# Two halves of a sequence solved together, and output work dealt over the merge, in a two-block network on one core

## The chip, the core and the metric

One core of a Trainium2 chip runs the whole program in one launch. The time is device microseconds of that core. The kernel before was timed in three runs. A profile was taken in one more execution; rows and busy times come from that one.

## The reference, cut to what matters

One sequence of 256 positions, width 1024, goes through two layers of a first kind and two of a second kind. The change touches the first kind only. Its layer, cut:

```python
u = rms_norm(h, norm_mix_g[layer])
p_a, p_b, p_c, p_gate = split(u @ w_in[layer])
y_a = rwkv7_branch(p_a, ...)     # per head: state = state*w + (state@a) b^T + v k^T ; y = state@r ; group norm
y_b = hgrn2_branch(p_b, ...)     # gated linear attention: scores with exp of cumulative gates; rms norm
y_c = dsa_branch(p_c, cos, sin)  # index scores, top 64 keys per query, softmax attention over them
branch = einsum('bsnc,ncd->bsnd', stack([y_a, y_b, y_c]), w_branch[layer])
merged = sum(sigmoid(p_gate) * branch, axis=2)
h = h + merged @ w_o[layer]
h = h + conv_glu(rms_norm(h, norm_ffn_g[layer]), ...)
```

The recurrence of the first branch is computed by halves c of 128 positions. For each head and half, a matrix I - N (N strictly lower triangular, from the keys and decays) has to be inverted, and the right sides of half 1 need the state that half 0 leaves.

## The kernel before, in words

Every engine has one queue in program order; semaphores join them. Weights stream in pieces of four blocks through a ring (SyncE's DMAs). ScalarE writes the high part of each piece into a ring of four (`hi.upto`, `hi.more`; L1325 is the line of all its activations), POOL subtracts to get the low part (L1291), and TensorE does three matmuls per block (`mm`, L650; transposes L759). A high part can be made only when the piece four before it is used, so ScalarE stands in `hi.upto` while TensorE is in a projection. PSUM banks are taken in the order of the list of `groups1`; each name waits for the one eight places before it.

One layer of the first kind, from the end of its first projections:

1. `scores(c)`: matrices N and T of half c. VectorE (from L2049) masks them into `nn`, `xd` and `zd`.
2. Levels k = 1 to 6 (`LEVELS` is 7), which double the inverted diagonal blocks: `level_first` (16 small matmuls per level), a copy by ScalarE (`level`, into `o1`), `level_second` (X and Z), a masked merge by VectorE (`level`, L2088 and L2091; L2083 in the last). `head_scores` with `take_scores` (L2068) make the scores of two heads beside levels 1 to 4.
3. `solve(c)`: right sides R, solutions SA, outputs Y, each with a copy by ScalarE between; for half 0 also the state ST, which VectorE scales in `state` (L2100, L2102) and on which R1 and Y1 rest.

Half 0 goes first. Beside its levels TensorE has the projections Bi, Cqi, Cki, Cv, Bg0, Bg1 and the rotations, and VectorE the rotary steps, the gate's logarithms and sums (L2183 to L2227) and the index scores. Then VectorE takes the top 64 keys (`take_best`, L2143 and L2144, eight rounds per block of queries; `best_mask`), and half 1 starts with `scores(1)`. Beside half 1's levels lie the attention (`logits`, `masked_logits` L2160 and L2162, `softmax`, `probabilities` L2168 and L2170, `turn_probs`, `values`), one unit of six per level, and the pair levels of the second branch: POOL's differences and products (`level_operands`, L1304, L1305, L1309, L1310), an exponential by ScalarE (`pair_decays`), `hgrn_pairs` on TensorE (banks H0 to H7) and `take_pairs` on VectorE (L2111 to L2116). POOL begins them after the low parts of Bg1. HO is that branch's output.

After that come the group means GM and the merge: for i = 0 to 11, over branches C, B, A with four column groups each, a gate projection and an output projection on TensorE, a sigmoid by ScalarE, a product and a sum by VectorE (L2286, L2289). The outputs of branch B (`yb`) and A (`ya`) get their norms and gains from VectorE (L1847 to L2277) before merge 0's product; their high and low halves must be there at merges 4 and 8.

## Time and profile before

| | us |
|---|---|
| median of three runs | 2082.19 |
| lowest and highest | 2081.07, 2087.68 |
| profiled execution | 2088.02 |
| its span | 2086.0 |
| TensorE busy | 1904.5 (91% of the span) |
| VectorE, ScalarE, POOL busy | 1288.3, 1145.3, 1032.5 |
| mean granted clock of TensorE | 0.953 of full speed |

The profile shows each instruction with its engine, line, start and duration in one execution. Idle time of an engine stands in brackets, with what ended it. A granted clock of 1.0 is 2.4 GHz and 0.5 is 1.2 GHz. In counts of instructions a small matmul of the program stands twice.

### The profile page before, as it was taken

What the parts mean: (1) busy time and instruction counts of PE and PEld (TensorE: products, weight loads), DVE (VectorE), ACT (ScalarE), POOL (GpSimd) and SP (SyncE); (2) the same over time, 40 slices, a digit from 0 to 9 for tenths busy, and PEclk for the clock granted to TensorE, in tenths of its full rate; (3) what the DMA queues carried; (4) which work ended last, traced back from release to release, by engine and by line L of the source; (5) the groups of instructions that cost most, each with busy time, mean ns of one, the idle gap of its engine ahead of it and who ended that gap; (6) DMA issues with size and microseconds to landing.
All of it is one profiled execution on the core that took longest, in us unless ns stands there. A gap on an engine that the chain in (4) does not pass through costs nothing.

```text
span 2086.0 us, 44562 instructions
## 1 busy us (share of the span) xinstructions
PE 1904.5 (91%) x16390; PEld 1795.9 (86%) x16390; DVE 1288.3 (62%) x1943; ACT 1145.3 (55%) x1928; POOL 1032.5 (49%) x742
## 2 busy tenths in 40 slices
PE   9897888999999898788999999988899998879999
PEld 8787777999999787677999989866799997659999
DVE  4567736369933367746268973476776536777754
ACT  5645255557755644355457655665655457465543
POOL 5662258929997572257938986751200045411000
PEclk9998799999999999799999999997999999879999
DMA  6332004656665442004656654530366653205665
GB/s 213 118 116 66 2 22 127 187 152 178 187 193 167 128 130 70 6 2 117 183 153 178 187 179 136 152 97 25 102 183 200 187 162 117 71 19 151 187 187 166
DMA packets 146923, 271.20 MB, mean 130 GB/s; under 512 B 16434, under 2 KB 16947, under 8 KB 146739
## 3 DMA queue, kind: packets, MB, share of 16 engines
q1 hardware_dynamic: 145296, 264.97, 43.5%
q10 hardware_dynamic: 1442, 3.66, 0.5%
q8 instruction: 130, 2.13, 0.4%
q14 instruction: 55, 0.44, 0.1%
HBM read 267.52 MB, written 1.05 MB: 129 GB/s over the span
## 4 chain that ended last, share of the span: by engine, by line
PE 68%; DVE 13%; ACT 10%; POOL 6%; issue 2%; ACTq 0%; DMA 0%; DVEq 0%; POOLq 0%
PE bank L650 67%; ACT arena L1325 7%; POOL ring_split L1291 5%; ACT hi_ring L1325 1%; DVE arena L1848 1%; PE bank L759 1%; DVE arena L1847 1%; DVE u L1918 1%; DVE arena L2144 1%; DVE small L2143 1%; ACT L1325 1%; DVE arena L2274 0%; DVE arena L2381 0%; DVE arena L2268 0%; DVE u_split L1923 0%
## 5 line engine op out<-in xcount | busy, mean ns | idle before, releaser
L1291 POOL TENSOR_TENSOR ring_split<-ring,hi_ring 128x512 fp32r<-128x512 f32 x682 | 961.9, 1435 | 742.1 <-ACT hi_ring L1325 731.9
L1325 ACT ACTIVATE hi_ring<-ring 128x512 fp32r<-128x512 f32 x1002 | 618.2, 630 | 520.9 <-PE bank L650 498.2
L650 PE MATMUL bank<-u_hi,hi_ring 128*128 128x256 f32 (+1 forms) x2480 | 678.6, 286 | 57.2 <-POOL ring_split L1291 44.7
L650 PE MATMUL bank<-u_split,hi_ring 128*128 128x256 f32 (+1 forms) x2480 | 667.0, 282 | 1.6 <-DVE u_split L1923 1.4
L650 PE MATMUL bank<-u_hi,ring_split 128*128 128x256 f32 (+1 forms) x2480 | 666.7, 281 | 0.0
L650 PEld LDWEIGHTS bank<-u_hi,hi_ring 128*128 128x128 f32 (+1 forms) x2480 | 454.5, 189 | 72.0 <-POOL ring_split L1291 50.8
L650 PEld LDWEIGHTS bank<-u_split,hi_ring 128*128 128x128 f32 (+1 forms) x2480 | 454.0, 189 | 4.1 <-DVE u_split L1923 2.4
L650 PEld LDWEIGHTS bank<-u_hi,ring_split 128*128 128x128 f32 (+1 forms) x2480 | 455.1, 189 | 1.0
L650 PE MATMUL bank<-arena 64*64 64x64 f32 (+6 forms) x3680 | 257.9, 266 | 51.3 <-ACT arena L1325 19.5
L650 PEld LDWEIGHTS bank<-arena 64*64 64x64 f32 (+3 forms) x3680 | 223.8, 163 | 91.3 <-issue 47.0
L1956 DVE TENSOR_TENSOR ring_split<-ring,hi_ring 128x512 fp32r<-128x512 f32 x320 | 217.6, 700 | 120.0 <-ACT hi_ring L1325 116.4
L650 PE MATMUL bank<-hidden_hi,hi_ring 128*128 128x256 f32 x864 | 242.9, 281 | 9.9 <-POOL ring_split L1291 9.9
L1325 ACT ACTIVATE arena<-bank 128x512 f32<-128x512 f32 (+5 forms) x262 | 131.6, 502 | 213.3 <-PE bank L650 171.9
L650 PE MATMUL bank<-hidden_hi,ring_split 128*128 128x256 f32 x864 | 242.1, 280 | 0.0
L650 PE MATMUL bank<-hidden_lo,hi_ring 128*128 128x256 f32 x864 | 242.1, 280 | 0.0
L1325 ACT ACTIVATE arena<-arena 128x1024 f32<-128x1024 f32 (+8 forms) x205 | 156.3, 763 | 44.5 <-DVE arena L2426 16.4
L650 PEld LDWEIGHTS bank<-hidden_hi,hi_ring 128*128 128x128 f32 x864 | 162.9, 189 | 11.6 <-issue 6.4
L650 PEld LDWEIGHTS bank<-hidden_hi,ring_split 128*128 128x128 f32 x864 | 165.3, 191 | 0.0
L650 PEld LDWEIGHTS bank<-hidden_lo,hi_ring 128*128 128x128 f32 x864 | 162.9, 189 | 0.0
L650 PE MATMUL bank<-arena,cst 128*128 128x256 f32 (+2 forms) x378 | 101.5, 412 | 13.6 <-ACT arena L1325 12.9
L1847 DVE SCALAR_TENSOR_TENSOR arena<-arena 128x1024 f32<-128x1024 f32 (+3 forms) x27 | 28.6, 1061 | 118.9 <-ACT arena L1325 118.6
L1325 ACT ACTIVATE arena<-bank,par 128x256 f32<-128x256 f32 x140 | 75.2, 537 | 43.7 <-PE bank L650 40.6
(247 smaller groups left out, 2445.3 us busy)
## 6 DMA issues: line engine op xcount, KB each, us to landing
ring<-in_stream SPq DMA_DIRECT2D x1002, 256.0 KB, 2.7
par<-in_params ACTq DMA_DIRECT2D x3, 637.0 KB, 4.3
h<-in_x SPq DMA_DIRECT2D x4, 256.0 KB, 4.1
cst<-in_cst SPq DMA_DIRECT2D x1, 993.0 KB
out<-h ACTq DMA_DIRECT2D x3, 256.0 KB, 2.8
par<-in_params ACTq DMA_DIRECT2D x1, 633.0 KB, 9.0
out<-h ACTq DMA_DIRECT2D x2, 128.0 KB, 2.3
msk<-in_masks SPq DMA_DIRECT2D x1, 104.0 KB
```

The source lines that it names most:

```text
L650: ins = nc.tensor.matmul(o, l, r, start=start, stop=stop)
L759: ins = nc.tensor.transpose(bank[:, i * P:(i + 1) * P], a, ident)
L1291: G.tensor_tensor(ring_lo[:, c, :], ring[:, c, :], hi_ring[:, q % HI_RING, :].bitcast(F32), ALU.subtract).then_inc(lo_by_pool, 1)
L1325: return nc.scalar.activation(o, i, f, **kw)
L1847: C.link(V.scalar_tensor_tensor(sq, sq, -0.5, y, ALU.mult, ALU.mult))
L1848: C.link(V.scalar_tensor_tensor(buf, sq, 1.5, buf, ALU.add, ALU.mult))
L1918: ins = V.scalar_tensor_tensor(u[:, k, :], h[:, k, :], gain[:, k:k + 1], buf, ALU.mult, ALU.mult)
L1956: V.tensor_tensor(ring_lo[:, c, :], ring[:, c, :], hi_ring[:, q % HI_RING, :].bitcast(F32), ALU.subtract).then_inc(lo_by_vector, 1)
L2143: C.link(V.max(m8, work[tt][:, 0:w]))
L2144: C.link(V.match_replace(work[tt][:, 0:w], m8, work[tt][:, 0:w], TAKEN))
```

## The change

Banks, instructions and results stay the same but for their order, with these differences. `nn`, `xd`, `zd`, `o1` and `x11` get a second buffer, in room that is free at the time, so both halves can be in levels at once. TensorE goes `scores(0)`, `scores(1)`, Bi, then per level both halves' `level_first`, the scores of two heads of half 0, both `level_second`, and the work beside. Index scores move from levels 4 and 5 to level 3, the gate's logarithms to before the levels (their activations before Bi on ScalarE), its sums to level 1, top-k of block 0 to level 4, pair group 7 and HT to level 5, HS and pair group 0 to level 6. After the levels come R0, SA0, Y0, ST, half 1's head scores, R1, SA1 and Y1, spread among attention units and pair levels, in an order written out by hand on each engine. The softmax maxima and sums get two sets of four columns. In the merge, the norm and gain work on `yb` follows merges 0 to 2 and that on `ya` merges 3 to 6, instead of all going before merge 0.

The core of the diff:

```diff
@@ groups1
+    beside = {1: ["Cqi", "Rq0", "Cki"], 2: ["Rq1", "Rk", "Cv", "Rqi", "Rki"], 3: [n for n, _, _ in INDEX] + ["Bg0"], 4: ["Bg1"], 5: ["HT", "H7"], 6: ["HS", "H0"]}
@@ build
+        nn = [nn0, v3(ya, 8)]
+        xd, x11 = ([v3(a[:, o:o + 512], 8) for o in (0, 512)] for a in (flat(xx), yb))
@@ tensor
                 scores(0)
+                scores(1)
                 project_rows(["Bi0", "Bi1"], u_parts, 4)
                 for k in range(1, LEVELS):
                     level_first(0, k)
+                    level_first(1, k)
+                    head_scores(0, pair_of(k))
                     level_second(0, k)
+                    level_second(1, k)
...
+                right_sides(0)
+                logits(0)
+                solutions(0)
+                logits(1)
+                hgrn_pairs(1)
+                outputs(0)
+                state()
+                turn_probs(0)
+                head_scores(1, (0, 1))
+                values(0)
+                hgrn_pairs(2)
+                turn_probs(1)
+                head_scores(1, (2, 3))
+                logits(2)
+                values(1)
+                head_scores(1, (4, 5))
+                logits(3)
+                head_scores(1, (6, 7))
+                hgrn_pairs(3)
+                turn_probs(2)
+                right_sides(1)
+                values(2)
+                logits(4)
+                turn_probs(3)
+                hgrn_pairs(4)
+                solutions(1)
+                values(3)
+                logits(5)
+                turn_probs(4)
+                hgrn_pairs(5)
+                outputs(1)
+                values(4)
+                turn_probs(5)
+                hgrn_pairs(6)
+                values(5)
@@ scalar
+                act.wait_ge(S["hcol_in"], past["hcol_in"] + 1)
+                C.link(A(lbc, lbc, ACT.Exp), S["hcol_out"])
+                act.wait_ge(S["ls_in"], past["ls_in"] + 1)
+                C.link(A(hE, bf, ACT.Abs))
+                C.link(A(hE, hE, ACT.Exp, scale=-1.0))
+                hi.more()
+                act.wait_ge(S["hcol_in"], past["hcol_in"] + 2)
+                nc.scalar.preload_act_table_set(LN)
+                C.link(A(lnA, lnA, ACT.Ln))
+                C.link(A(ln1m, ln1m, ACT.Ln), S["hcol_out"])
+                C.link(A(hE, hE, ACT.Ln, bias=1.0), S["ls_out"])
                 for t in range(NT):
                     hi.upto("Bi0")
...
+                take_sides(0)
+                softmax(0)
+                take_solutions(0)
+                softmax(1)
+                take_outputs(0)
+                pair_decays(2)
+                take_turned(0)
+                take_values(0)
+                pair_decays(3)
+                take_turned(1)
+                take_values(1)
+                softmax(2)
+                softmax(3)
+                pair_decays(4)
...
@@ vector
+                C.link(V.tensor_tensor(lbc, p("lb0"), p("lb1"), ALU.subtract), S["hcol_in"])
+                C.link(V.tensor_scalar(hls, bf, 0.0, None, ALU.min), S["ls_in"])
                 C.link(V.memset(st, 0.0))
                 C.link(V.memset(hsc, 0.0))
                 scores(0)
+                lower_bounds()
+                scores(1)
+                gate_logs()
                 for k in range(1, LEVELS):
+                    take_scores(0, pair_of(k))
+                    for c in range(2):
+                        level(c, k, 0)
+                        level(c, k, 1)
...
+                masked_logits(0)
+                take_best(1, half_rounds // 2)
+                masked_logits(1)
+                take_best(1, half_rounds // 2)
+                probabilities(0)
+                take_pairs(1)
                 state()
+                take_scores(1, (0, 1))
+                probabilities(1)
+                take_pairs(2)
+                take_scores(1, (2, 3))
+                take_best(1, half_rounds // 2)
+                best_mask(1)
+                masked_logits(2)
...
@@ the merge on vector, after the product and sum of merge i
+                    if i == 0:
+                        refine(C, "hgrn", 2)
+                    elif i == 1:
+                        C.link(V.tensor_tensor(yb, yb, hE, ALU.mult))
+                        dve.wait_ge(S["bsg_ready"], past["bsg_ready"] + 1)
+                        gated(C, (0, 1))
+                    elif i == 2:
+                        gated(C, (2, 3))
+                        split(C, yb, yb_hi, yb_lo, S["yb_ready"])
+                    elif i == 3:
+                        refine(C, "rwkv", 3)
+                    elif i == 4:
+                        C.link(V.tensor_tensor(ya, ya, ysq, ALU.mult))
+                        gained_groups(C, (0, 1))
+                    elif i == 5:
+                        gained_groups(C, (2, 3))
+                        C.link(V.tensor_tensor(ya, ya, bonus, ALU.add))
+                    elif i == 6:
+                        dve.wait_ge(S["gA_ready"], past["gA_ready"] + 2)
+                        C.link(V.tensor_tensor(ya, ya, gA, ALU.mult))
+                        split(C, ya, ya_hi, ya_lo, S["ya_ready"])
```

## Rows read from the trace of the kernel before

**Rows 1.** Stretches: us, busy (instructions) PE, PEld, DVE, ACT, POOL, clock, DMA share, GB/s.

```profile
121.70:200.20 78.50, 69.41 (x864) 62.71 (x864) 49.69 (x102) 36.62 (x59) 31.15 (x25) 0.93 0.30 89
200.20:224.87 24.67, 16.04 (x172) 14.91 (x169) 18.16 (x56) 7.87 (x14) 0.86 (x1) 0.69 0.03 10
224.87:283.98 59.11, 49.48 (x865) 43.32 (x865) 39.05 (x83) 26.25 (x63) 31.74 (x25) 0.87 0.01 2
283.98:300.90 16.92, 15.55 (x144) 13.53 (x145) 4.35 (x3) 6.31 (x10) 7.81 (x6) 0.90 0.01 1
311.50:423.00 111.50, 101.43 (x819) 98.78 (x818) 56.42 (x43) 58.78 (x91) 95.30 (x65) 0.98 0.54 157
...
835.20:859.80 24.60, 16.04 (x170) 14.89 (x169) 18.15 (x56) 7.82 (x14) 0.86 (x1) 0.68 0.03 9
```

**Rows 2.** Waits of TensorE, 121.7 to 301 us: total us, times, longest.

```profile
PE bank L650 <- ACT arena L1325: 9.8, 7, 2.9
```

**Rows 3.** Timeline of VectorE between the halves: start us, duration, engine, line, operation.

```profile
206.96 0.29 DVE L2143 MAX8 small<-arena 128x8 f32<-128x128 f32 x1
...
213.54 0.43 DVE L2143 MAX8 small<-arena 128x8 f32<-128x256 f32 x1
...
217.48 0.43 DVE L2049 COPY arena<-cst 128x512 f32<-128x512 f32 x1
```

**Rows 4.** Timeline of TensorE: pair matrices, level groups, Bg1, half 1's start, pairs.

```profile
121.70 2.06 PE L650 MATMUL bank<-arena 64*128 64x128 f32 x32
...
149.38 2.08 PE L650 MATMUL bank<-arena 64*64 64x64 f32 x64 [0.76 <-ACTq L271]
...
169.64 1.15 PE L650 MATMUL bank<-arena 64*64 64x64 f32 x32 [0.18 <-DVE arena L1930]
...
190.46 0.41 PE L650 MATMUL bank<-u_hi,ring_split 128*128 128x256 f32 x1
...
224.87 12.76 PE L650 MATMUL bank<-arena 64*64 64x64 f32 x192 [5.03 <-DVEq L271]
...
280.43 1.15 PE L650 MATMUL bank<-arena 128*64 128x64 f32 x32
```

**Rows 5.** Timeline of VectorE: a pass over 1024 columns, probabilities, masked logits.

```profile
160.28 1.76 DVE L2200 TENSOR_SCALAR arena<-arena 128x1024 f32<-128x1024 f32 x1
...
257.47 1.52 DVE L2170 TENSOR_TENSOR arena<-arena,small 128x512 f32<-128x512 f32 x1
...
265.58 0.69 DVE L2160 SCALAR_TENSOR_TENSOR arena<-bank,arena 128x512 f32<-128x512 f32 x1 [0.37 <-PE bank L650]
```

**Rows 6.** Timeline of ScalarE: a table load, two small logarithms, one over 1024 columns.

```profile
157.74 1.28 ACT L1556 ACT_TABLE_LOAD   x1
159.03 0.44 ACT L1325 ACTIVATE small<-small 128x4 f32<-128x4 f32 x2
...
173.11 1.06 ACT L1325 ACTIVATE arena<-arena 128x1024 f32<-128x1024 f32 x1
```

**Rows 7.** Timeline of POOL: one pair level (differences, products) and the next one's start.

```profile
273.45 1.04 POOL L1304 TENSOR_TENSOR arena<-arena 128x512 f32<-128x512 f32 x1
...
276.76 1.26 POOL L1309 TENSOR_TENSOR arena<-arena 128x512 f32<-128x512 f32 x1 [1.24 <-ACT arena L1325]
...
279.32 1.37 POOL L1304 TENSOR_TENSOR arena<-arena 128x512 f32<-128x512 f32 x1
```

**Rows 8.** POOL's low parts (L1291) in two stretches: us, busy (pieces), clock, DMA, GB/s.

```profile
325.00:348.00 23.00, 22.01 (x12) 1.00 0.49 137
352.00:402.00 50.00, 46.72 (x36) 0.97 0.61 176
```

**Rows 9.** Waits of TensorE in the merge, 311.5 to 423: total us, times, longest.

```profile
PE bank L650 <- POOL ring_split L1291: 9.9, 11, 3.0
```

**Rows 10.** Timeline of VectorE in the merge: first step on yb, merge 0's product.

```profile
315.24 1.23 DVE L1847 SCALAR_TENSOR_TENSOR arena<-arena 128x1024 f32<-128x1024 f32 x1 [10.70 <-ACT arena L1325]
...
348.23 0.69 DVE L2286 TENSOR_TENSOR arena<-bank,arena 128x512 f32<-128x512 f32 x1
```

More of the change, by code:

```diff
@@ L535, in build @@
         ya = pa[:, 0:4, :].rearrange("p a t -> p (a t)")
+        nn = [nn0, v3(ya, 8)]
+        xd, x11 = ([v3(a[:, o:o + 512], 8) for a in (flat(xx), yb)] for o in (0, 512))
         merged = ar.rearrange("p j a t -> p (j a t)")
@@ L1605, in take_turned @@
                     B.release(act, f"CP{b}")
-                for i in range(LEVELS - 1):
-                    level(1, i + 1)
-                    if i > 1:
-                        take_values(i - 2)
-                    pair_decays(i)
-                    softmax(i)
-                    if i:
-                        take_turned(i - 1)
-                pair_decays(LEVELS - 1)
-                take_values(len(ATT1) - 2)
-                take_turned(len(ATT1) - 1)
-                take_values(len(ATT1) - 1)
+                act.wait_ge(S["hcol_in"], past["hcol_in"] + 1)
@@ new lines, in _ @@
+                for t in range(NT):
+                    hi.upto("Bi0")
+                    bank = B.wait(act, f"Bi{t}")
+                    C.link(A(bi[:, t, :], bank[:, :], ACT.Copy), S["bi_ready"])
+                    B.release(act, f"Bi{t}")
+                for k in range(1, LEVELS):
+                    level(0, k)
+                    level(1, k)
+                    if k == 1:
+                        act.wait_ge(S["lse_in"], past["lse_in"] + 1)
+                        C.link(A(hks, hks, ACT.Exp))
+                        hi.more()
+                        C.link(A(hE, hE, ACT.Abs))
+                        C.link(A(hE, hE, ACT.Exp, scale=-1.0))
+                        nc.scalar.preload_act_table_set(LN)
+                        hi.more()
+                        C.link(A(hE, hE, ACT.Ln, bias=1.0), S["lse_out"])
+                        take_raw("Cqi", 4, 2)
+                        take_raw("Cki", 6, 1)
+                    elif k == 2:
+                        hi.upto("Cv")
+                    elif k == 3:
+                        act.wait_ge(S["cum_b"], past["cum_b"] + 1)
+                        b8 = v3(hb, 8)
+                        for hd in range(4):
+                            C.link(A(v3(hke, 4)[:, hd, :], b8[:, 2 * hd, :], ACT.Exp, scale=-1.0, bias=b8[:, 2 * hd, P - 1:P]))
+                        C.link(A(v3(hqe, 4), b8[:, 1:8:2, :], ACT.Exp), S["d_exp"])
+                    if 3 <= k <= 4:
+                        g = k - 3
+                        hi.upto(f"Bg{g}")
+                        bank = B.wait(act, f"Bg{g}")
+                        C.link(A(bsg[:, g * 512:(g + 1) * 512], bank[:, :], ACT.Copy))
+                        B.release(act, f"Bg{g}")
+                    elif k == 5:
+                        pair_decays(0)
+                        bank = B.wait(act, "HT")
+                        C.link(A(ketm, bank[:, :], ACT.Copy), S["ketm_ready"])
+                        B.release(act, "HT")
+                    elif k == 6:
+                        pair_decays(1)
+                        bank = B.wait(act, "HS")
+                        C.link(A(hst.rearrange("p (a t) -> p a t", a=4), v3(bank[:, :], 4), ACT.Copy), S["hstate_ready"])
+                        B.release(act, "HS")
@@ L1619, in _ @@
+                pair_decays(5)
+                take_turned(3)
+                softmax(4)
+                take_solutions(1)
+                take_values(3)
+                softmax(5)
+                pair_decays(6)
+                take_turned(4)
+                take_outputs(1)
+                take_values(4)
+                take_turned(5)
+                take_values(5)
                 hi.upto(MERGE[0][0], 0)
-                solve(1)
                 C.link(A(bsg, bsg, ACT.Silu), S["bsg_ready"])
@@ new lines, in gate_sums @@
+                def gate_sums():
+                    dve.wait_ge(S["lse_out"], past["lse_out"] + 1)
+                    C.link(V.tensor_tensor(hls, hls, hE, ALU.add))
+                    for j in range(4):
+                        C.link(V.tensor_scalar(v3(hks, 4)[:, j, :], v3(hks, 4)[:, j, :], omlb[:, j:j + 1], None, ALU.mult))
+                    for i in range(8):
+                        C.link(V.tensor_tensor_scan(v3(hb, 8)[:, i, :], ones, v3(hls, 8)[:, i, :], 0.0, ALU.mult, ALU.add))
+                    dve.sem_inc(S["cum_b"], 1)
```

336 lines of the change are left out of this document (125 added, 211 removed).

## The prediction

> **What bounds the kernel now.** I read the busy table of the page first: TensorE is busy nine tenths of the span, so a gain has to come from its idle time, from matmuls at the low clock, or from both. The strip of 40 slices shows where: slices 4 and 5 (TensorE 7 and 8 tenths, hardly any DMA) and 17, the solves of the two layers of the first kind. The table of stretches comes next [rows 1]. From the pair matrices (121.7) to the first group means (300.9) the first layer spends 78.50 + 24.67 + 59.11 + 16.92 = 179.2 us, with TensorE busy 150.5 of it and a mean granted clock of 0.93, 0.69, 0.87 and 0.90. The second layer repeats it (24.60 us for 24.67), so I work out one layer and double. The table of waits says that TensorE waits here for copies of ScalarE most (9.8 us in 7 waits [rows 2]), then for VectorE, and hardly for weights. VectorE's order of time explains the 24.67 us: eight rounds of top-k and the mask for block 0 from 206.96, four rounds for block 1 from 213.54, half 1's start from 217.48 [rows 3], then the state; TensorE's first level of half 1 starts at 224.87 after 5.03 us of idle time [rows 4]. After that each level of half 1 takes some 7 to 8 us, though its two groups of matmuls take 1.15 and 2.08 us. Last, the merge: 111.5 us [rows 1], with 9.9 us of waits, all on POOL's low parts [rows 9].
>
> **The change part by part, one layer.**
>
> **First stretch (78.50 us).** Half 1's pair matrices (2.06 us), its levels (five of 1.15 + 2.08, the last about 1.14), the transposes of HT (0.66), HS (about 0.5, as those transposes less a part) and two groups of pair levels (1.15 each, the row at 280.43) join it [rows 4]: 2.06 + 17.3 + 0.66 + 0.5 + 2.3 = 22.8 us of TensorE. It now idles 78.50 - 69.41 = 9.1 us here, and 27 matmuls of Bg1, after the idle time before them, run at the low clock (0.41 us one [rows 4]), at a step of 0.21 instead of 0.12 us: 2.6 us more. Each half's matmuls now lie in the other's copy and merge, so I let these 11.7 us go. Two new stalls come. The gate's logarithms move before Bi: ScalarE then waits for lower_bounds, which VectorE does after scores(0) (near 130.5, since a min over 1024 columns, the 1.76 us of L2200, now goes ahead of it too [rows 5]); the table and three logarithms take 1.28 + 0.44 + 1.06 [rows 6]. Queued behind are the high parts of Bi, of which four exist; TensorE is through with them at about 131.6 and gets the fifth at 133.5 + 0.63 + 1.27, 3.8 us of stall. The other: top-k of block 0 with its mask (213.54 - 206.96 = 6.6 us [rows 3]) is queued on VectorE behind level 4, and level 5's merge behind it; Bg1 (5.9) covers all but about 2.4 us. What VectorE gains here (scores(1) 6.0 us, from 217.48 to the state, half 1's merges some 7, top-k 6.6 and two rounds 2.0, pair takes and the like 3.5) brings it from 49.7 to 75 us, under TensorE. Sum: 78.5 - 11.7 + 22.8 + 6.2 = **96 us**; without any gap-filling it would be 78.5 + 22.8 = 101.
>
> **The 24.67 us** go as a stretch: no wait for top-k stands before a level. What they hold for TensorE (R0, SA0, Y0, ST) moves into the next.
>
> **Second stretch.** I laid the four queues beside each other in the new order, with these durations. VectorE: six masked logits at two passes of 0.69, six probabilities at 0.7 to 1.52 [rows 5], six pair takes at about as much, four score takes at 1.02, six rounds at (217.48 - 213.54)/4 = 0.98 [rows 3], mask and state 2.2: 36 us. TensorE: today's 16.04 + 49.48 + 15.55 us of busy time [rows 1], less the 22.8 that moved and HO's 3.5, is 54.8 at a mean clock of about 0.8; I count 32 at the full one. The pair levels: POOL's two differences take 2.1 us, ScalarE's exponential 1.06, POOL's products 2.5; a round without other waits is 5.9 us [rows 7], and level 2 can start only at about 2 us after the first stretch ends, since level 1 waits for H0. Five rounds are then 30 us, and ScalarE's fixed order (pair_decays(4) behind softmax(3), which waits for VectorE's mask of block 1) adds about 6 and the start and H6 about 8. Laid out, the last take_pairs falls 46 us after the first stretch. What is late last is the pair chain with VectorE's attention steps, no longer the levels. Bounds: VectorE's 36 us below, today's 59.11 above (then the rounds keep today's pace). I take 46.
>
> **Tail (16.92 us).** R1, SA1 and Y1 (three round trips to ScalarE) now lie among attention; HO is left, 3.5 us.
>
> By this the layer takes 96 + 46 + 3.5 = 145.5 for 179.2, 33.7 us less. The layout assumes that every wait ends as soon as it can and that TensorE keeps the full clock, while it would be busy 32 of 46 us; in today's second stretch it is busy 49.5 of 59.1 and gets 0.87. I add 7 us: 4 for matmuls at the half clock (about 9 of the 32 us), 3 for waits that I didn't see. **Saved: 26.7 us per layer.**
>
> **Merge.** VectorE's work on yb and ya, 33 us from 315.24 to the first gate product at 348.23 [rows 10], is today a stretch of its own in which POOL needs 22.01/12 = 1.83 us per piece for 46.72/36 = 1.30 otherwise [rows 8]. It is dealt over merges 0 to 6. The 816 matmuls of the stretch need 96.1 us at a step of 0.118; it takes 111.5, so 15.4 are to be had. Stay: about 4 us of the first stalls, from ScalarE's roots before the high parts. Go: the last and longest stall of 3.0 us [rows 9] and the half clock after it (1.9), since gate 2's product no longer waits for ya. Between them: the same VectorE work costs POOL 33 x (1 - 1.30/1.83) = 9.6 us, but now 59 us of TensorE's steps have 59 x (1.41 - 1.30)/1.41 = 4.6 us of slack. A turn of VectorE has 4 to 6 us of work in 8.5 us, and yb and ya come about 7 us before branches B and A want them, so no wait is added there. I take 8 us saved; ends 3 and 11.
> POOL's pieces stretch in the rows wherever VectorE works on two arena operands. The Trainium skill, page "SBUF — State Buffer", section "Who interferes with whom", makes this an exclusive lock: a VectorE instruction with two SBUF inputs and a GpSimd one that reads SBUF block each other. That speaks against this edit: the same instructions collide wherever they stand, and dealing them out would save only the last stall. It is the third rival below.
>
> **Sum.** 2 x (26.7 + 8) = 69.4 us. The profiled execution took 2088.02 us, 2.0 of them outside its span; 2088.0 - 69.4 = 2018.6. The median of the runs shown is 5.8 us lower than the profiled one, so the forecast is **2013 us**.
>
> **The rivals.**
> First, **the layout holds in full**: 33.7 + 11 per layer, 2082.2 - 89.4 = 1993 us. For it: the serial top-k is plainly gone. Against it: ScalarE's order is fixed, and each late step delays those behind it.
> Second, **today's pace stays**: a round of attention and pairs costs what it does now, because the queues wait for each other in turn (the levels were only the visible part): second stretch 60, first 100, tail 4, saved 15; merge 5. 2082.2 - 40 = 2042 us. For it: rounds of 7 to 8 us now, where POOL's own is 5.9.
> Third, **the merge gains only its last stall or less**: 2082.2 - 2 x 26.7 = 2029 us.
> Fourth, **nothing much**: the halves don't cover each other, as one queue (VectorE with 75 us of work and a dozen waits) sets the first stretch, which grows by what the rest gives: 2082 us.
> Fifth, **slower by the clock**. TensorE's work in the two stretches, 90 + 32 us, is cut into short groups; today the granted clock falls to 0.50 (1.2 GHz) after idle time, as in Bg1 from 189.87 to 195.6 [rows 4], and a matmul then takes 1.8 times as long. From 43 us of that work at the half clock on (34.7/0.8) the gain is gone; with half of the work, 61 us, a layer loses 49 - 34.7 = 14: 2110 us. Against it: the first stretch, with fewer gaps to fill, has 0.93 today.
> The Trainium skill, page "TensorE: Matmul & The Clock Gate", section "What's actually happening", says that the throttled state is the default and that activity releases it; the 0.69 of the 24.67 us agrees, and by it the change should raise the clock on the whole.
>
> **Chances.** Forecast 0.49, full layout 0.17, merge without gain 0.14, today's pace 0.12, nothing 0.04, slower 0.04. The range takes in the first four cases but for the ends: 1988 to 2043. A measurement can tell about 0.3% from no change: faster 0.92, same 0.04, slower 0.04.
>
> **What would show it.** Right: half 1's first level beside half 0's, no idle of 5 us before a level, 93 to 100 us for the first stretch and 46 to 54 for the second, the stall in Bi, no VectorE stretch of 33 us in the merge and about 103 us for it. Wrong: a first stretch over 105 us, a granted clock under 0.8 in the second, POOL pieces of 1.8 us through seven merges. The work after the merge should not move.

## The result, and the profile after

The changed kernel takes 2051.3 us (median of four; 2044.0 to 2054.8) beside 2084.8 for the kernel before in the same session: a ratio of 0.984, 95% interval 0.982 to 0.986. That is 33 us less, with an interval of 29 to 38. Timed again later it gave 0.985 (0.983 to 0.988). The forecast was 69.4 us less: the sign was right, and the time lies 8 us above the range.

The profiled execution has a span of 2046.5 us, 39.5 less than before. Read at landmarks, 35.2 of these lie where the change is: 14.5 and 13.7 between the first pair matrix and the group means (the two layers), 3.3 and 3.7 in the merge. The remaining 4.3 are the sum of small differences in code that did not change (the part behind layer 2's merge took 1017.1 us in this execution and 1024.7 in that of before); other executions differ there as much. So the change is worth 17.6 us per layer in this profile (15.7 in a second one, `changed_again` below) where 34.7 were forecast.

The stretches of the changed kernel, to be held against [rows 1]: levels of both halves, attention with outputs, group means to second gate, merge; then the second stretch in layer 2 (columns: us; busy and instructions of PE, PEld, DVE, ACT, POOL; granted clock; DMA share; GB/s).

```profile
122.37:219.22 96.85, 87.32 (x1439) 80.07 (x1438) 74.78 (x168) 45.55 (x81) 39.13 (x29) 0.96 0.26 75
219.22:287.04 67.82, 53.33 (x600) 46.27 (x601) 38.51 (x78) 29.02 (x62) 32.79 (x26) 0.87 0.01 1
287.04:297.69 10.65, 10.65 (x74) 10.05 (x73) 1.38 (x2) 8.01 (x12) 4.25 (x4) 1.00 0.34 100
297.69:405.70 108.01, 101.64 (x818) 99.57 (x817) 58.58 (x43) 58.86 (x91) 96.91 (x65) 0.97 0.57 161
...
838.27:907.67 69.40, 54.92 (x600) 47.28 (x601) 38.49 (x78) 29.02 (x62) 32.78 (x26) 0.83 0.01 2
```

The first stretch is 96.85 us where 96 were forecast. The 24.67 us are gone. The second stretch with its tail is 67.8 and 69.4 where 56.5 were forecast, at a granted clock of 0.87 and 0.83. The merge fell from 111.3 to 108.0 and not to 103.5. TensorE's waits between 121 and 300 us (total, times, longest) were on ScalarE's copies most of all before [rows 2]; now they are on VectorE:

```profile
PE bank L758 <- DVE arena L2212: 12.6, 5, 6.1
PE bank L649 <- DVE arena L2109: 5.2, 2, 4.2
PE bank L649 <- POOL ring_split L1317: 3.7, 2, 3.5
...
PE bank L649 <- ACT arena L1351: 0.9, 3, 0.4
```

L2212 is the last step of `probabilities`, L2109 is `take_scores`, L1317 the low parts. TensorE's timeline shows where (in brackets the idle time before):

```profile
135.49 0.50 PE L649 MATMUL bank<-hi_ring,u_hi 128*128 128x512 f32 x1 [3.48 <-POOL ring_split L1317]
...
169.36 1.97 PE L649 MATMUL bank<-arena 64*64 64x64 f32 x32 [4.19 <-DVE arena L2109]
171.26 3.74 PE L649 MATMUL bank<-arena,cst 128*128 128x256 f32 x8
...
252.55 1.11 PE L758 MATMUL bank<-cst,arena 128*128 128x128 f32 x4 [6.14 <-DVE arena L2212]
253.46 8.04 PE L649 MATMUL bank<-arena 128*128 128x128 f32 x36
264.04 1.11 PE L758 MATMUL bank<-cst,arena 128*128 128x128 f32 x4 [2.54 <-DVE arena L2212]
265.08 5.88 PE L649 MATMUL bank<-arena 128*64 128x64 f32 x76
273.50 0.86 PE L758 MATMUL bank<-cst,arena 128*128 128x128 f32 x4 [2.54 <-DVE arena L2212]
```

Four transposes take 1.11 us at 252.55 and 264.04, and 0.66 at the full clock: the granted clock falls to 0.50 (1.2 GHz) in the idle time at 249.9, and TensorE starts the next work with it. What VectorE did in the 6.14 us before CP2:

```profile
244.03 1.08 DVE L2191 TENSOR_SCALAR arena<-arena 128x256 f32<-128x256 f32 x1
245.14 1.22 DVE L2192 TENSOR_TENSOR arena<-arena,cst 128x256 f32<-128x256 f32 x1
246.39 0.69 DVE L2201 SCALAR_TENSOR_TENSOR arena<-bank,arena 128x512 f32<-128x512 f32 x1
247.23 0.69 DVE L2203 TENSOR_REDUCE small<-arena 128x2 f32<-128x512 f32 x1
247.95 1.02 DVE L2109 TENSOR_TENSOR arena<-bank,cst 128x384 f32<-128x384 f32 x2
248.89 0.68 DVE L2201 SCALAR_TENSOR_TENSOR arena<-bank,arena 128x512 f32<-128x512 f32 x1
249.72 0.69 DVE L2203 TENSOR_REDUCE small<-arena 128x2 f32<-128x512 f32 x1
250.44 1.02 DVE L2109 TENSOR_TENSOR arena<-bank,cst 128x384 f32<-128x384 f32 x2
...
251.80 0.69 DVE L2212 TENSOR_TENSOR arena<-arena,small 128x512 f32<-128x512 f32 x1
```

It had no pause. The mask of block 1 (L2191, L2192) ends only at 246.4, and between masked_logits(2) and the probabilities(2) that TensorE waits for stand two score takes, the next unit's masked logits and two more score takes, as the order is written by hand.

### The profile page after: what moved, and what is told of

It reads as the page before. It is cut to its first block, busy times and chain, and to the rows that moved or that the text cites. A ratio compares the mean times of both kernels' runs of the same rounds, so it can differ in the third digit from the quotient of the medians.

```text
span 2046.5 us, 44566 instructions
## 1 busy us (share of the span) xinstructions
PE 1883.6 (92%) x16390; PEld 1778.9 (87%) x16390; DVE 1293.0 (63%) x1943; ACT 1140.5 (56%) x1924; POOL 1037.9 (51%) x742
## 4 chain that ended last, share of the span: by engine, by line
PE 65%; DVE 15%; ACT 9%; POOL 8%; issue 3%; DMA 0%; ACTq 0%; DVEq 0%; SPq 0%
PE bank L649 63%; POOL ring_split L1317 8%; ACT arena L1351 7%; ACT hi_ring L1351 1%; PE bank L758 1%; DVE arena L1891 1%; DVE u L1961 1%; DVE arena L1890 1%; DVE arena L2062 1%; DVE arena L1975 1%; DVE arena L1974 0%; DVE arena L2109 0%; DVE arena L1973 0%; ACT L1351 0%; DVE arena L2464 0%
## 5 line engine op out<-in xcount | busy, mean ns | idle before, releaser
L1317 POOL TENSOR_TENSOR ring_split<-ring,hi_ring 128x512 fp32r<-128x512 f32 x682 | 969.1, 1449 | 736.7 <-ACT hi_ring L1351 730.9
L649 PE MATMUL bank<-arena 64*64 64x64 f32 (+6 forms) x3680 | 240.3, 255 | 14.6 <-DVE arena L2109 9.3
L649 PEld LDWEIGHTS bank<-arena 64*64 64x64 f32 (+3 forms) x3680 | 210.4, 155 | 49.5 <-issue 29.7
L649 PE MATMUL bank<-arena,cst 128*128 128x256 f32 (+2 forms) x378 | 105.4, 424 | 13.6 <-ACT arena L1351 12.9
L649 PEld LDWEIGHTS bank<-arena,cst 128*128 128x128 f32 (+2 forms) x378 | 72.1, 203 | 29.9 <-ACT arena L1351 16.6
```

The lines of the kernel that those rows point to most:

```text
L649: ins = nc.tensor.matmul(o, l, r, start=start, stop=stop)
L1317: G.tensor_tensor(ring_lo[:, c, :], ring[:, c, :], hi_ring[:, q % HI_RING, :].bitcast(F32), ALU.subtract).then_inc(lo_by_pool, 1)
```

## The experiments

All runs in one table. "Solve" is the time from the first pair matrix to the group means, "merge" that from the second gate group to the first matmul of the output projection, each for layers 1 and 2, read from TensorE's timeline in the profiled execution. (The stretch to 405.70 above stops 3.3 us short of that matmul.)

| kernel | ratio to before, 95% | solve | merge |
|---|---|---|---|
| before | 1 | 179.2, 179.1 | 114.6, 114.9 |
| changed | 0.984 (0.982 to 0.986) | 164.7, 165.5 | 111.3, 111.1 |
| changed_again | 0.985 (0.983 to 0.988) | 168.6, 165.5 | 111.2, 111.1 |
| merge_alone | 0.998 (0.996 to 0.999) | 177.8, 177.9 | 111.1, 111.3 |
| solve_alone | 0.990 (0.988 to 0.992) | 168.6, 165.4 | 114.6, 114.5 |
| gate_later | 0.986 (0.984 to 0.988) | 165.5, 165.2 | 111.1, 111.2 |
| bi_parts | 0.986 (0.984 to 0.989) | 168.1, 165.6 | 111.2, 111.3 |
| mask_sooner | 0.981 (0.978 to 0.984) | 160.8, 155.6 | 111.3, 111.1 |
| warm | 0.984 (0.981 to 0.987) | 159.0, 160.4 | 111.1, 111.1 |
| roots_between | 0.984 (0.982 to 0.987) | 164.3, 165.5 | 109.8, 109.8 |
| four | 0.980 (0.977 to 0.982) | 158.1, 155.6 | 109.7, 109.8 |
| best_solve | 0.977 (0.974 to 0.979) | 160.0, 157.6 | 109.8, 109.8 |
| share | 0.984 (0.981 to 0.987) | 166.7, 164.6 | 109.5, 110.1 |
| no_norm | 0.982 (0.978 to 0.985) | 160.6, 164.5 | 104.6, 107.0 |
| warm_order | 0.976 (0.973 to 0.978) | 154.6, 155.6 | 109.8, 109.8 |
| warm_share | 0.979 (0.976 to 0.981) | 159.2, 158.9 | 109.4, 109.6 |
| warm_best | 0.975 (0.973 to 0.978) | 157.1, 153.6 | 110.6, 109.0 |

A difference of 0.003 between two ratios is not settled by the times; the landmarks of the merge are sharper, as an unchanged order repeats there to 0.3 us; the solve does not repeat so well (164.7 and 168.6 for the same kernel).

### The two parts apart

`merge_alone` is the kernel before with the dealt merge:

```diff
-                refine(C, "hgrn", 2)
-                ...
-                split(C, ya, ya_hi, ya_lo, S["ya_ready"])
                 for i, (_, output, _, j) in enumerate(MERGE):
                     ...
+                    if i == 0:
+                        refine(C, "hgrn", 2)
+                    elif i == 1:
+                    ...
```

> The kernel before with one part of the change alone: VectorE's work on yb and ya is dealt over merges 0 to 6; the solves are as before. My prediction gave this part 8 us per layer, 16 in all. Dealing theory as the changed kernel's profile now reads: the merge goes from 111.3 to about 108 us, 3.3 per layer, because what is saved in the middle is partly lost at its start, where ScalarE's roots stand before the first gate and a stretch at the half clock follows: 6 to 7 us in all, ratio 0.997. Rival (my prediction's own size): the start costs what it costs because of the lockstep solve and not because of the dealing, so alone it saves 16 us, ratio 0.992. Second rival, the lock: VectorE's and GpSimd's instructions collide wherever they stand, GpSimd's pieces stay at 1.83 us beside VectorE's work, and the merge gains 3 us or less by its last stall alone.

`solve_alone` is the changed kernel with that edit undone.

> The changed kernel with the merge of before: the 33 us of VectorE's work on yb and ya stand as one block before the first gate product. If the parts add up, solve and merge alone save together the 33 to 36 us of the whole change. By the profiles the solve saves 14.5 us per layer (179.2 to 164.7), 29 in all, ratio 0.986, and the merge reads 111 us again. If the two parts help each other (the dealt merge needs outputs early, or the start of the merge is hurt by the lockstep), the sum of the two savings is off by more than 5 us.

By the landmarks the parts add. The merge alone gives 3.5 us per layer, the lockstep solve alone 10.6 and 13.7, 31.4 us together; the whole change gives 31.4 in `changed_again` and 35.2 in the first profile, whose solve of layer 1 was 3.9 us shorter. The merge reads 111.1 with either solve; `merge_alone`'s solve is 1.3 us shorter than before in both layers, for which I have no cause. The times say less: the parts save 5.5 and 19.9 us, 25 together, for 29 to 33 of the whole, and that 4 to 8 us is near what their intervals allow. POOL's low parts in the merge, before (first line), in `merge_alone` (second) and in the changed kernel (third): count, busy us, mean ns, idle before.

```profile
L1291 POOL TENSOR_TENSOR ring_split<-ring,hi_ring 128x512 fp32r<-128x512 f32 x65 | 95.3, 1487 | 16.2 <-ACT hi_ring L1325 13.5
```

```profile
L1291 POOL TENSOR_TENSOR ring_split<-ring,hi_ring 128x512 fp32r<-128x512 f32 x65 | 97.0, 1530 | 11.0 <-ACT hi_ring L1325 11.0
```

```profile
L1317 POOL TENSOR_TENSOR ring_split<-ring,hi_ring 128x512 fp32r<-128x512 f32 x65 | 96.9, 1526 | 11.2 <-ACT hi_ring L1351 10.9
```

The 65 pieces did not become cheaper; what went is 5 us of POOL's idle time, the 3.0 us stall of [rows 9] with it (TensorE's longest wait in the merge is now 2.0 us). And the half clock at the merge's start costs at most 0.2 us: the changed kernel has it in layer 1 and `merge_alone` has not (clock 0.77 against 1.00 in the 15 us after the first stall), and they take the same time. In layer 2 it is the other way round (mean clock of the merge 1.00 and 0.97, 111.1 and 111.3 us).

```profile
303.40:318.50 15.10, 12.09 (x77) 11.68 (x78) 5.17 (x3) 9.67 (x14) 10.96 (x8) 0.77 0.37 105
```

```profile
316.00:331.00 15.00, 10.82 (x84) 10.05 (x85) 5.16 (x3) 10.46 (x15) 10.87 (x8) 1.00 0.36 106
```

### One wait at a time in the first stretch

`gate_later` moves the eight scans of `gate_sums` behind level 2's first rotations, `bi_parts` gives Bi two more high parts ahead of the wait for lower_bounds:

```diff
@@ gate_later, VectorE, level 2
                         rotate("Rk", 7, 2)
+                        gate_scans()
                         bank = B.wait(dve, "Cv")
@@ bi_parts, ScalarE
                 hi.more()
+                hi.more()
+                hi.more()
                 act.wait_ge(S["hcol_in"], past["hcol_in"] + 2)
```

> The changed kernel with the eight scans of the gate's sums moved on VectorE: they come after the rotations of level 2, where VectorE waits 2.98 us for the bank Cv, and not between level 1's rotations and level 2's masks. Queue theory: TensorE's 4.19 us stall at 169.36 (its wait for L2109, queued behind the scans) goes, and with it the 7 us at a granted clock of 0.5 that follow (10 matmuls of 128x256 at 0.48 for 0.24 us): 4 + 2.5 = 6.5 us per layer, 13 in all, against the changed kernel. Rival, the work theory: VectorE's scans (4.1 us) only move to another stretch of TensorE's path and are waited for there (Rki's rotation, the index scores): 0 to 4 us in all. Slower if cum_b comes too late for the first pair level: the H0 and HT groups then wait.

> The changed kernel with two more high parts of Bi's weights on ScalarE ahead of its wait for lower_bounds. Queue theory: TensorE's wait of 3.48 us in Bi (135.49) falls to 0.5 to 1 us, as two pieces carry it for 2.9 us; the logarithms start about 0.5 us later, which nobody waits for: 2.5 us per layer, 5 in all. Rival: the two pieces delay the logarithms, VectorE's gate_logs (136.61) and with them level 1's masks, so that the wait comes back in level 1: 0 us.

Both gave nothing that the landmarks can tell (`gate_later` 0.2 to 0.8 us in the first stretch). In `gate_later` the wait of 4.19 us is 0.41, but TensorE now waits for VectorE a little later, 2.16 and 1.08 us, and the half clock comes there (0.72 in 175 to 187 us, for 0.66 in 165 to 175):

```profile
165.07 1.15 PE L649 MATMUL bank<-arena 64*64 64x64 f32 x32 [0.41 <-DVE arena L2109]
178.97 1.48 PE L649 MATMUL bank<-arena 64*128 64x256 f32 x8 [2.16 <-DVEq L271]
181.53 2.72 PE L649 MATMUL bank<-arena 64*64 64x64 f32 x46 [1.08 <-DVE arena L1973]
```

VectorE has no pause over 0.3 us from 165 to 183 us, so the scans are free nowhere in it, and most of their 4 us was still waited for, only later. In `bi_parts` the wait shrank by 0.9 us, from 3.48 to 2.59, not by 2.5; TensorE then ran at the half clock in Bi and level 1's wait grew from 0.96 to 1.32 us. The half clock there need not come of the edit: `changed_again`, without it, has it from 132.7 to 139.5 us, and the profile of the changed kernel shown above has not.

### Order, clock, and both, in the second stretch

`mask_sooner` changes VectorE's order only; `warm` changes no order and puts dummy matmuls into three waits:

```diff
@@ mask_sooner, VectorE (level 5: take_best(1, half_rounds) for half of that)
                 probabilities(1)
+                best_mask(1)
                 take_pairs(2)
                 take_scores(1, (2, 3))
-                take_best(1, half_rounds // 2)
-                best_mask(1)
                 masked_logits(2)
                 take_scores(1, (4, 5))
                 masked_logits(3)
-                take_scores(1, (6, 7))
                 probabilities(2)
+                take_scores(1, (6, 7))
@@ warm, TensorE, in turn_probs
+                    if 2 <= i <= 4:
+                        keep_warm(B.open(pe, f"CP{b}"), 16 if i == 2 else 6)
                     pe.wait_ge(S["probs_ready"], past["probs_ready"] + i + 1)
```

> The changed kernel with VectorE's order mended in the second stretch: two of block 1's rounds of top-k go back to level 5, the mask of block 1 comes right after probabilities(1), and probabilities(2) ahead of take_scores of heads 6 and 7. Queue theory: masked_logits(2) starts some 3.4 us sooner (its bank is full at 241.9, it started at 246.39), CP2's wait of 6.14 us falls to 1 to 2 us, and the granted clock, which fell to 0.50 after it, stays up: 4 us of wait and 3 to 5 us of matmuls at the half clock, 7 to 9 us per layer, 14 to 18 in all. Rival, what is late next: the round trip CP, CO, pairs on ScalarE and the two groups at ScalarE's order hold the next steps all the same: 0 to 2 us per layer. Second rival, the clock falls anyway, since TensorE is idle in short pieces from 235 on: 4 us per layer, 8 in all.

> The changed kernel with dummy matmuls (128x256, 0.24 us each at the full clock) on the bank that is waited for: 16 before CP2, 6 before CP3 and 6 before CP4, about 3.8, 1.4 and 1.4 us inside waits of 6.14, 2.54 and 2.54 us. Nothing else moves. Clock theory: TensorE's work from 252.55 to 280 ran at a granted clock of 0.50 to 0.88; kept busy, it keeps 1.0, and the 27 us shrink by 4 to 6 per layer, 8 to 12 in all, though no wait is taken away. Rival, waits only: what ends the steps are VectorE and ScalarE; a faster TensorE waits longer, and the added matmuls cost what they overrun: within 2 us, or up to 3 us slower.

The dummies alone shorten the solve. `warm`'s second stretch, and the group of its dummies (each stands twice in the count; they take 12.9/28 = 0.46 us each, where I had expected 0.24):

```profile
218.50:281.69 63.19, 59.09 (x657) 50.99 (x658) 38.54 (x78) 29.02 (x62) 32.81 (x26) 1.00 0.01 2
```

```profile
L649 PE MATMUL bank<-cst 128*128 128x256 f32 x56 | 12.9, 383 | 0.8 <-DVEq L271 0.8
```

63.2 us at clock 1.00, although the dummies overran the first wait (CP2 comes 253.54 - 218.50 = 35.0 us into the stretch, for 252.55 - 219.22 = 33.3). One stretch is little, as the clock differs from layer to layer and execution to execution with the same instructions. Over all kernels that keep this stretch's order there are sixteen without dummies, with clocks of 0.80 to 0.89 and 63.8 to 71.5 us, 69.0 on average, and four with dummies (`warm` and `warm_share`), all at 1.00 and 62.3 to 63.2 us, 62.7 on average. Keeping the full clock saves 6.3 us per layer, with what the dummies overran already paid. `warm`'s own times (ratio 0.984) do not show its 5 to 6 us per layer; those rest on the profiles. A second pair of kernels shows the gain in the times too: `share` has 0.984 (0.981 to 0.987), and `warm_share`, which adds dummies here and four in the merge, 0.979 (0.976 to 0.981).

The same rows give TensorE's work here at the full clock: 59.1 - 12.9 = 46.2 us, or 43.3 without HO (2.9 us at 278.90), which the prediction has in its tail. The prediction counted 32.

`mask_sooner` took the wait at CP2 from 6.14 to 1.49 us. Its layers differ by how far the clock fell, the second being near what the mechanism promised:

```profile
218.18:282.32 64.14, 53.77 (x601) 45.95 (x601) 37.59 (x78) 29.02 (x62) 32.73 (x26) 0.87 0.01 2
833.71:893.15 59.44, 48.73 (x601) 41.85 (x602) 37.58 (x78) 29.03 (x62) 32.72 (x26) 0.97 0.01 2
```

`four` joins `mask_sooner`, `gate_later`, `bi_parts` and `roots_between` (below); `best_solve` is `four` without `bi_parts`, with dummies: 3 before CP2, 5 before CP3 and CP4, and 4 before the index scores.

> The changed kernel with four edits at once: the gate's scans later, two more high parts ahead of the logarithms, block 1's mask sooner with probabilities(2) ahead of take_scores of heads 6 and 7, and high parts between the steps of the merge's roots. If every queue theory holds they add up to 6.5 + 2.5 + 7 + 5 = 21 us per layer, 42 in all, and the kernel comes to about 2010 us, which is where the prediction was. If each mended wait is replaced by the next one, it comes to 2040 or more.

> The changed kernel with the mask of block 1 sooner and probabilities(2) ahead of take_scores of heads 6 and 7, the gate's scans later, high parts between the steps of the merge's roots, and dummy matmuls (0.46 us each at the full clock by the profile of the kernel with dummies: 56 records, 12.9 us for 28) inside the waits: 4 before the index scores, 3 before CP2, 5 each before CP3 and CP4. Clock theory: the first stretch loses its 9 us at half clock (175 to 187), the second its 25, so pair matrices to group means take 153 to 156 us in both layers alike, against 164.7 and 165.5; with 1.4 us from the merge that is 10 to 13 us per layer, about 2027 us. Rival, waits only: the dummies change nothing and it reads as the four edits together did, 158 us and 2035.

By the landmarks `four` gave 19 us of the 42 expected: the edits to the first stretch count for nothing, and the clock still falls. `best_solve` missed its 153 to 156 us in both layers. Its 4 dummies before the index scores filled no wait (their bank came free too late: the 2.16 us stand as before), and its first stretch is 2.4 and 2.2 us longer than `four`'s. In layer 2 the clock stayed at 1.00 through the second stretch (59.3 us); in layer 1, with the same instructions, it fell at 240.1, before the first of the other dummies and after short waits that had none:

```profile
235.00:245.00 10.00, 7.19 (x65) 5.29 (x62) 9.11 (x16) 2.91 (x5) 8.42 (x8) 0.75 0.01 2
```

`warm_order` (`mask_sooner` with `roots_between`) fills all of them from 234 us on: 1 dummy before CP0 and CP1, 2 before H2, 3 before CP2, 5 before CP3 and CP4.

> The changed kernel with the mask of block 1 sooner, probabilities(2) ahead of take_scores of heads 6 and 7, high parts between the steps of the merge's roots, and dummy matmuls in every wait of the second stretch from its first on: 1 before CP0 and CP1, 2 before H2, 3 before CP2, 5 each before CP3 and CP4. The version with four edits and fewer dummies lost the clock at 240, before its first dummy. Clock theory: with no gap left from 234 on the granted clock stays 1.00 to the group means; then the order's gain (4 us) and the clock's (5 us) add, and pair matrices to group means take 154 to 157 us in both layers (164.7 and 165.5 before), about 2025 us. Rival, waits only: the dummies' time is lost where the mended order has taken the waits away, 158 to 160 us.

Order and clock add. Its second stretch in both layers:

```profile
218.42:276.06 57.64, 55.64 (x635) 46.51 (x636) 37.63 (x77) 29.03 (x62) 32.72 (x26) 1.00 0.01 2
828.62:886.59 57.97, 55.63 (x634) 46.51 (x635) 37.60 (x77) 29.02 (x62) 32.72 (x26) 1.00 0.01 2
```

Both layers have 1.00 and lie within 1.1 us in the solve. 57.6 and 58.0 us is 1.1 and 1.5 more than the prediction gave the second stretch and tail (56.5). The first stretch, to which two rounds of top-k moved, pays hardly anything for it: 97.0 and 97.7 us, for 96.9 and 96.1 in the changed kernel and 95.8 and 97.3 in `warm`.

### What sets the merge

These runs have the changed kernel timed again beside them (`changed_again`). `roots_between` lets ScalarE make high parts between the steps of its two roots (`weights=hi` in both calls of `rstd`); `share` gives VectorE the low parts of all twelve output projections; `no_norm` leaves out most of the dealt work, so its output is not the reference's:

```diff
@@ share
-BY_VECTOR1 = {"A second", "WO", "U second"}
+BY_VECTOR1 = {"A second", "WO", "U second"} | {m[1] for m in MERGE}
@@ no_norm, VectorE: the dealt steps of merges 0 to 6 but these
+                    if i == 2:
+                        split(C, yb, yb_hi, yb_lo, S["yb_ready"])
+                    elif i == 6:
+                        split(C, ya, ya_hi, ya_lo, S["ya_ready"])
```

> The changed kernel with high parts of weights set between the steps of ScalarE's two roots at the start of the merge (after the copies, after the logarithm, after the exponential) instead of behind each root. Queue theory: the stalls of TensorE at 303.41, 309.93 and 312.56 (1.13 + 2.02 + 0.98 us, all on GpSimd's low parts, whose high parts stand behind the roots) fall to 1 us or less, and the 6 us at a granted clock of 0.52 after them cost nothing more (29 matmuls in 5.94 us for 3.5): 5 us per layer, 10 in all. Rival, GpSimd bounds the merge: it is busy in 22.3 of 22.5 us from 318.5 on, at 1.39 us per piece, and 65 pieces at that rate are 90 us of the 108: a better start is kept, unless its low parts are the later ones anyway; then 0 to 4 us in all.

> The changed kernel itself, timed beside the next three on one chip so that they can be compared with it directly. Expected: 2046 to 2055 us and a ratio of 0.984 to the kernel before, with landmarks in its profile within 1 us of the first profile (pair matrices to group means 164.7 and 165.5 us in the two layers, merge to the output projection 111.2).

> The changed kernel with the low parts of the weights of all twelve output projections of the merge (24 of about 65 pieces per layer) made by VectorE instead of GpSimd. GpSimd theory: the merge is set by GpSimd's queue (busy 97 of 108 us, in every version of it the same 111.2 us from the second gate to the output projection, at full and at half clock alike); with 41 pieces left, about 61 us of work, TensorE's own 96 us of matmuls and the start's roots set it: 103 to 105 us for 111.2, 6 to 8 us per layer, 12 to 16 in all. Rival, VectorE's turn: with two more pieces of 0.7 to 1.2 us each in a turn that has 4 to 6 us of dealt work beside the product and the sum, VectorE is late in merges 1 to 6, and the merge stays at 111 or grows. Rival, clock and roots: the merge's loss is at its start, where nothing changes: within 2 us.

> The changed kernel without most of the work that was dealt over the merges: the refinement of the two inverse roots, their products with ya and yb, the gains, the bonus and the gate are left out, and only the two splits into high and low parts stay, so the output is not the reference's. This measures what that work costs GpSimd. Collision theory: GpSimd's pieces fall from a mean of 1.49 us (97 us for 65) to about 1.3, its queue to 86 us, and the merge from 111.2 to 102 to 105 us: the work costs the merge 6 to 9 us per layer wherever it stands, which is what my prediction took for saved. Rival, no price: pieces stay near 1.49 us and the merge at 110 or more, since hand-overs and not VectorE slow them.

`no_norm` (first two lines) and `share` (the other two), their merge in layer 1 and POOL's pieces in it:

```profile
293.03:397.67 104.64, 100.52 (x835) 99.39 (x833) 31.98 (x32) 59.49 (x92) 88.78 (x65) 1.00 0.60 172
...
L1317 POOL TENSOR_TENSOR ring_split<-ring,hi_ring 128x512 fp32r<-128x512 f32 x65 | 88.8, 1401 | 12.7 <-ACT hi_ring L1351 11.4
```

```profile
298.76:408.22 109.46, 103.35 (x834) 101.02 (x833) 66.92 (x73) 59.48 (x92) 62.00 (x41) 0.98 0.59 164
...
L1317 POOL TENSOR_TENSOR ring_split<-ring,hi_ring 128x512 fp32r<-128x512 f32 x41 | 62.0, 1517 | 37.4 <-ACT hi_ring L1351 35.3
```

The changed kernel repeated itself but for the solve of layer 1, 168.6 for 164.7, with a granted clock of 0.81 for 0.87 in its second stretch. Without the dealt work POOL needs 8.1 us less and the merge 6.6 (4.1 in layer 2, where the clock was 0.85 from 907 to 930 us, for 1.00 all through layer 1): dealt out, the work still costs POOL nearly the 9.6 us that I had reckoned for the block. Against the kernel before, `no_norm`'s merge is 10.0 and 7.9 us shorter, so dealing it out saves a third to a half of what it costs. `share` took 35 us off POOL, and the merge lost only 1.8 and 1.0 us. So POOL's queue is not alone in setting it: VectorE's own pieces take 0.9 us each, TensorE now waits 2.0 us for one of them, and the start keeps its 4.1 us of waits on POOL. `roots_between` took 1.4 us off the merge, not 5: the waits went from 8 of at most 2.0 us (6.2 together) to 11 of at most 1.0 (6.0 together). The last two runs tell whether the merge's edits and the solve's add.

> The changed kernel in its own order with dummies before CP2, CP3 and CP4 (14, 6 and 6), the merge's output weights' low parts made by VectorE, and 4 dummies before gate group 2 of the merge. Solve: as with dummies alone, 159 to 160.5 us from the pair matrices to the group means. Merge: with VectorE's share it read 109.5 and 110.1 us at a granted clock of 0.93 and 0.84 in its first 20 us; if the clock is what is left there, it now reads 106 to 108, and the kernel 2030 to 2035 us. Rival: the merge's start is set by ScalarE's roots, whatever the clock, and stays at 109.5.

> All of it at once: the sooner mask, roots with high parts between their steps, VectorE's share of the low parts, two more high parts in Bi, dummies in the second stretch's waits (1, 2, 4, 6, 6 before CP0 to CP4, 3 before H2) and 4 before gate group 2. If solve and merge are as separate as the runs with one part alone say, this adds up: 154 to 158 us for pair matrices to group means and 105 to 107 for the merge, 2015 to 2020 us. Rival: in the merge the two edits feed the same slack, since with high parts between the roots GpSimd's queue was the bound and with VectorE's share the start was: 108, and 2025 us or more.

In `warm_share` the merge's clock is 1.00 throughout and it takes 109.4: with VectorE's share too, the half clock was not what was left. In `warm_best` the solve is where its sum had it (157.1 and 153.6), but VectorE's late pieces come to 4.6 us in three waits, and the merge stays at 110.6 and 109.0: the merge's edits don't add. The forecast's 8 us less would read 106.6 in the table. What would bring the merge there I have not found; only leaving work out did (104.6, and 107.0 in layer 2).

`warm_order` and `warm_best` beat both kernels: 0.976 (0.973 to 0.978) and 0.975 (0.973 to 0.978), 2025 and 2027 us beside 2074.

## Why the prediction was right or wrong

**First stretch: right.** 96 forecast, 96.85 measured, the stall in Bi 3.48 for 3.8. Its inside differs: the 2.4 us at level 5 didn't come (the mask of block 0 ends at 211.7, just ahead of level 5's merges), and one of 4.19 us at level 2 did, where `gate_sums` (8.3 us of VectorE from 159.66) stands ahead of the takes. I had let TensorE's own 11.7 us of old gaps and half clock go completely; some of it came back in this form.

**The 24.67 us: right**, they went.

**Second stretch and tail: wrong, 56.5 against 67.8 and 69.4.** Three things failed. First the layout, "I take 46", with 3.5 for the tail: `warm_order`, with the clock kept and VectorE's order mended, still takes 57.8 us, 8.3 above these 49.5. "I count 32" in it is wrong: the rows behind it (54.8 us at a mean clock of about 0.8) give 44, and the measured work is 43.3. So the layout saw TensorE idle for 14 of its 46 us, which is 3 by the measured work. How much of the 8.3 us comes of this no run takes apart. Second, the allowance of 7 us. Its clock term, 4 us for 9 of the 32 us at the half clock, measures 6.3 (69.0 against 62.7 us). Its term for unseen waits, 3 us, was too small because I took the queues as if each wait ended as soon as it could, and did not write VectorE's order from 240 to 252 beside TensorE's: `warm_order` takes 4.9 us off `warm`'s and `warm_share`'s 62.7. Clock and order together are 11.2 us per layer, and the layout's own 8.3 more than use up the 7 that were allowed: 49.5 + 8.3 + 11.2 = 69.0. Third, POOL's pair chain, named as what is late last, is not: POOL idles 9.56 us for TensorE before its products at 267.24.

**Merge: wrong, 8 against 3.3 and 3.7.** The step that failed is "I take 8": I set POOL's 9.6 us of stretched pieces against slack in the rest of the merge. The mean of all 65 pieces is no lower after than before (1526 and 1487 ns, 1.6 us more in all), so nothing of POOL's work was saved. Only its idle time could shrink, and that went from 16.2 to 11.2 us, about the 4.6 us of slack that I had reckoned; POOL was already busy 46.72 of 50 us in the later part [rows 8]. The third rival's mechanism held: the merge gained little more than the 3.0 us of its last stall, though its 2029 us counts nothing at all for the merge. What I thought saved is what `no_norm` finds still paid, 6.6 and 4.1 us.
On the Trainium skill, page "SBUF — State Buffer", section "Who interferes with whom": the direction agrees. Taking 61.74 - 31.98 = 29.8 us of VectorE's time out of the merge freed 8.1 us of POOL's. That is 0.27 us per us. The page calls the shared ports an exclusive lock; these rows don't say how much of VectorE's work had two inputs in SBUF or stood beside a piece, so they neither bear out nor refute a full block.

**The rivals.** The second, today's pace at 2042, was nearest, though for another reason: its 15 us per layer match the 14.5 and 13.7 of the solve, and with 3.3 for its 5 in the merge the sum is 2 x 18.3 = 36.6, 2046. The fifth, slower by the clock, had the right mechanism: the granted clock falls to 0.50 in the wait at CP2. It had the wrong size, 6.3 us per layer where 34.7 were needed to lose the gain: the stretch kept a mean clock of 0.80 to 0.89, and the first stretch 0.96. I gave the second 0.12 and the third 0.14 as if only one could hold, while both came true together: their common case, 2046, was in neither.
The Trainium skill, page "TensorE: Matmul & The Clock Gate", section "What's actually happening", on activity as what lifts the throttle: the four stretches with dummies agree, at 1.00 each. But from it I had concluded that the change "should raise the clock on the whole". It rose from 0.953 to 0.959 in the profiles, as one trough was exchanged for several small ones.

## What to carry to other kernels

When two chains are laid side by side, write the whole queue of the engine that serves both in order, with durations, between each pair of its customer's steps: the wait was in VectorE's hand-written order and not in any engine's sum. Take an engine's work at the full clock from the rows by count and duration, never as what remains of a layout. In the second stretch a wait on TensorE cost twice, itself and the half clock after it; dummy matmuls won the second part back. How many it takes these runs leave open: three filled waits kept 1.00 in all four stretches of the old order, fewer dummies in the mended order kept it in one layer of `best_solve` and lost it in the other, and filling every gap kept it in both layers of `warm_order` and `warm_best`. It pays only where TensorE, and not another queue, sets the pace.

## What the runs showed of the hardware

The granted clock differs between executions of identical instructions (0.80 to 0.89 in the second stretch, 63.8 to 71.5 us), so a landmark in one profile carries luck unless the clock is read beside it (3.9 us between the two profiles of the changed kernel). In the merge, a clock of 0.77 over 15 us cost at most 0.2 us, where POOL was busy for 97 of 111 us; one of 0.80 to 0.89 over the second stretch cost 6.3. And taking 24 of 65 pieces from POOL left its mean at 1.52 us for the other 41: a piece's duration there goes with what VectorE does beside it (1.40 in `no_norm`), not with the length of POOL's queue.
